# Experts' gate and up weights of a megabyte per transfer, their places released and awaited two pieces at a time

## The chip, the cores and the metric

One core of a Trainium2 chip runs the whole program in one launch. The metric is the device time of one execution in microseconds (us), the median over runs. The engines of the core are TensorE (PE; its weight loads are listed as PEld), VectorE (DVE), ScalarE (ACT), GpSimd (POOL) and SyncE (SP). Sixteen DMA engines move data between HBM and the core's SBUF; nearly all transfers of this kernel are issued by SP, in one queue.

## What is computed

The reference runs two blocks over 256 rows of width 1024, in float32. The first block has two layers, a retention mixer and a block attention mixer, each followed by a mixture of experts. The second has four layers (differential attention, HGRN2, chunked gating, differential attention), each with a cross attention and a dense SwiGLU. The change touches only the two mixtures of experts:

```python
def hier_moe(x, w_rg, b_rg, w_re, b_re, w_gate, w_up, w_down):
    ...                       # a router picks one of 4 groups and 2 of its 4 experts per row
    combine = (group_w[:, :, None] * within[:, None, :]).astype(x.dtype)
    y = jnp.zeros_like(t)
    for g in range(G):
        hg = jax.nn.silu(jnp.einsum('td,edf->tef', t, w_gate[g])) * jnp.einsum('td,edf->tef', t, w_up[g])
        y = y + jnp.einsum('tef,efd->td', hg * combine[:, g, :, None], w_down[g])
    return y.reshape(B, S, D)
```

Each layer has 16 experts with three matrices of 1024 by 512 numbers. All 16 experts' weights are read in each layer, 100.7 MB of float32, since some row may want any of them.

## The kernel before, in words

**Weights.** All "wide" weights come as blocks of 1024 by 512 numbers (2 MB). A block lies in HBM as four pieces (`WP = 4`), each 128 rows of 1024 numbers: 4 KB for each of the 128 partitions, 512 KB in all. In HBM the four pieces of a block stand one behind another, so that the same partition's rows of two neighbouring pieces are 512 KB apart. In SBUF a block fills 16 KB of each partition, piece behind piece. A "down" block is two such pieces (1 MB).

**Outside the experts** a block goes to `stage_w`, is split by ACT (`high_w`, line 748) and DVE (`low_w`, line 1179) and is then multiplied by PE (lines 2075 to 2077). SP issues a piece of the next block when the split has released the place (line 554).

**In a mixture of experts** the rows chosen by each expert are gathered, at most 64 for each (function `sparse`; another branch, `every`, takes over when an expert has more, and it does not run with these inputs). Experts go in 8 pairs, and the 512 hidden columns of an expert are done in two halves, so a layer has 16 steps, `v` = 0 to 15. A step needs, for both experts of the pair, the gate and up block of that half (`wide`, 4 MB together) and the down block (2 MB together). There are two sets of places: even steps use `proj` and `stage_w` (with `proj` and `stage_d` for down), odd steps `pair_w` and `pair_d`. PE does, in this order and in every step, `wide(v)` (line 2351; piece by piece, both experts side by side), inside it the transposes of the previous step's hidden values (line 2366) after the first piece, and in odd steps from 3 on a scatter (lines 2414 and 2415) before the third piece; then `down(v-1)` (line 2379). In early steps a gather (lines 2301 to 2310) and small products that weigh the slots (line 2326) follow.

**Order of the transfers.** SP works through one list written out by hand: in each layer `wide(v)` for v = 0 and 1 with their down blocks, then for v = 2 to 15 `wide(v)` and behind it, from v = 3 on, `down(v-1)`, then `down(15)`, then the first block of the stage that follows the experts, into `stage_w` (`load_wide` with `behind`). A transfer into a place waits until PE has used what lay there: `used_mw[i]` counts the pieces that PE has finished for expert `i`. For v = 0 and 1 the places belonged to the stage before, and the waits are on the splits (`split_lw`) or on PE (`used_w`). PE waits for a piece on `landed_mw[u][p]`, one semaphore for each piece number and each set, 16 for each expert's transfer. After the last step ACT and DVE split the first two pieces of the block that follows (lines 748 and 1179) before they keep the last pair's results (lines 878 and 1518), which PE then scatters (lines 2414, 2415) and DVE adds to `h` (line 1528).

`keep_clock` (line 2070) is a run of products whose result nobody reads.

Of the kernel before, what the change touches and what calls it, by code (L numbers as in the profile page):

```python
# [33 lines left out]
PIECE = 1024  # L34
WP = KC * WIDE // PIECE
# [23 lines left out]
PAIRS = ALL // 2  # L59
HALVES = MOE_UNITS // PAIRS // 2  # L60
# [213 lines left out]
def scatter_at(v):  # L274

    return (v - 3) // HALVES if v % HALVES and v >= 3 else None
# [38 lines left out]
def build(nc, dram, out):  # L315
    ctx = ExitStack()
    with ctx:
# [3 lines left out]
        def sem(name):  # L321
            return ctx.enter_context(nc.semaphore(name))
# [75 lines left out]
        def moe_wide(u, i):  # L398

            if u == 0:  # L400
                return stage_w[:, :] if i else proj[:, 0:WP * PIECE]
            return pair_w[i][:, :]
# [7 lines left out]
        def moe_x(r):  # L410
            return qk[:, 0:KC * S] if r % 2 == 0 else proj[:, X0:X0 + KC * S]
# [64 lines left out]
        split_hw, split_lw = sem("split_hw"), sem("split_lw")  # L476
        split_hd, split_ld = sem("split_hd"), sem("split_ld")
        used_w, used_d = sem("used_w"), sem("used_d")
# [38 lines left out]
        landed_mw = [[sem(f"landed_mw{u}{p}") for p in range(WP)] for u in range(HALVES)]  # L517
        landed_md = [[sem(f"landed_md{u}{p}") for p in range(DP)] for u in range(HALVES)]
        used_mw = [sem(f"used_mw{i}") for i in range(2)]
# [25 lines left out]
        def _(sp):  # L545
# [26 lines left out]
            def units_of(m, v):  # L572
                return [MOE_UNITS * m.moe + 2 * HALVES * (v // HALVES) + HALVES * i + v % HALVES for i in range(2)]

            def load_pair_wide(m, v, experts=range(2)):
                u, unit = v % HALVES, units_of(m, v)
                step, last = STEPS * m.moe + v, m.wide - 1
                for p in range(WP):
                    for i in experts:
                        if v >= HALVES:  # L580
                            sp.wait_ge(used_mw[i], WP * (step - HALVES) + p + 1)
                        elif u:
                            sp.wait_ge(used_w, WP * last + p + 1)
                        elif i:
                            sp.wait_ge(split_lw, WP * last + p + 1)
                        sp.dma_start(moe_wide(u, i)[:, p * PIECE:(p + 1) * PIECE],
                                     dram["wide"][m.wide + unit[i], p, :, :]).then_inc(landed_mw[u][p], 16)

            def load_pair_down(m, v, experts=range(2)):
                u, unit = v % HALVES, units_of(m, v)  # L590
# [11 lines left out]
            for s in PLAN:  # L602

                if s.kind == "residual" and moe_of(s) is not None:
                    m = PLAN[PLAN.index(s) + 3]
# [1460 lines left out]
        def _(pe):  # L2066
# [204 lines left out]
            def sparse(s):  # L2271
# [58 lines left out]
                def wide(v):  # L2330
                    q, u = v // HALVES, v % HALVES
                    e = q if q < 2 else q // 2 * 2 + 1
                    if v >= 2:
                        pe.wait_ge(way.gated, v - 1)
                    for p in range(WP):
                        if v == 0:
                            pe.wait_ge(way.first_kept, p + 1)
                        elif p == 0 and e:
                            pe.wait_ge(way.x_left, e)
                            pe.wait_ge(way.x_right, e)  # L2340
                        if v and p == 1:
                            turn_hidden(v - 1)
                        if p == 2 and scatter_at(v) is not None:
                            scatter(scatter_at(v), v)
                        pe.wait_ge(landed_mw[u][p], 32 * (PAIRS * s.moe + q + 1))
                        for k in range(KP):
                            c = KP * p + k
                            for i in range(2):
                                half = slice(i * SLOTS, (i + 1) * SLOTS)
                                x = c * S + q % 2 * P + i * SLOTS  # L2350
                                mm = pe.matmul(bank[4 + v % 2][half, :], moe_x(q // 2)[:, x:x + SLOTS],  # L2351
                                               moe_wide(u, i)[:, c * WIDE:(c + 1) * WIDE], start=c == 0, stop=c == KC - 1)
                                if k == KP - 1:
                                    mm.then_inc(used_mw[i], 1)
                        if v == 0 and p + 2 < WP:
                            gather_first(p + 2)

                def turn_hidden(v):
                    pe.wait_ge(way.gated, v + 1)
                    if v:  # L2360
                        pe.wait_ge(way.kept, v)
                    if v == 1:
                        pe.wait_ge(way.weights_kept, 1)
                    for c in range(DP):
                        o = GATED0 + FU + c * P
                        mm = pe.transpose(bank[6][:, c * P:(c + 1) * P], qk[:, o:o + P], ident[:, :])
                    mm.then_inc(way.turned, 1)
# [33 lines left out]
                def scatter(q, v):  # L2401
                    n = issued(gather_at, v)
                    pe.wait_ge(way.x_left, n)
                    pe.wait_ge(way.x_right, n)
                    pe.wait_ge(way.slots_kept, issued(turn_at, v))
                    if q:
                        pe.wait_ge(way.added, 4 * q)
                    for i, (t, half, b) in enumerate(scatter_order(q)):
                        if t == 0:
                            pe.wait_ge(way.z_low, 2 * q + half + 1)  # L2410
                        if i == 3 and q < PAIRS - 1:
                            pe.wait_ge(way.added, 4 * q + 1)
                        chosen = slots(q)[:, t * P:(t + 1) * P]
                        pe.matmul(b[:, :], chosen, z_high(half), start=True, stop=False)
                        pe.matmul(b[:, :], chosen, z_low(half), start=False, stop=True).then_inc(way.scattered, 1)
# [19 lines left out]
            def every(s):  # L2435
                way = ways[s.moe]
                steps = STEPS * s.moe

                def unit(q, u, i):
                    n = 2 * u + i  # L2440
                    for t in range(T):
                        x = slice(t * P, (t + 1) * P)
                        for p in range(WP):
                            pe.wait_ge(landed_mw[u][p], 32 * (q + (PAIRS * s.moe + 1)))
                            for k in range(KP):
                                c = KP * p + k
                                w = moe_wide(u, i)[:, c * WIDE:(c + 1) * WIDE]
                                pe.matmul(bank[4 + t][:, :], xhv[:, c, x].bitcast(F32), w, start=c == 0, stop=False)
                                mm = pe.matmul(bank[4 + t][:, :], xlv[:, c, x].bitcast(F32), w, start=False,
                                               stop=c == KC - 1)  # L2450
                            if t == T - 1:
                                mm.then_inc(used_mw[i], 1)
                    pe.wait_ge(way.gated, 2 * (2 * HALVES * q + (n + 1)))
                    for c in range(DP):
                        for t in range(T):
                            mm = pe.transpose(bank[6][:, c * S + t * P:c * S + (t + 1) * P],
                                              y[:, 512 + t * FU + c * P:512 + t * FU + (c + 1) * P], ident[:, :])
                    mm.then_inc(way.turned, 1)
                    pe.wait_ge(way.kept, 2 * HALVES * q + (n + 1))
                    for p in range(DP):  # L2460
                        pe.wait_ge(landed_md[u][p], 32 * (q + (PAIRS * s.moe + 1)))
                        for t in range(T):
                            for half in range(2):
                                mm = pe.matmul(bank[2 * t + half][:, :],
                                               qk[:, p * S + t * P:p * S + (t + 1) * P],
                                               moe_down(u, i)[:, p * PIECE + half * WIDE:][:, 0:WIDE],
                                               start=p == 0, stop=p == DP - 1)
                        mm.then_inc(used_md[i], 1)
                    pe.wait_ge(way.added, 4 * (2 * HALVES * q + (n + 1)))

                with pe.Fori(0, PAIRS) as q:
                    for u in range(HALVES):
                        for i in range(2):
                            unit(q, u, i)
# [466 lines left out]
```

## Time and profile before

| | us |
|---|---|
| median of 3 runs | 2607.13 (2606.32 to 2611.19) |
| the profiled execution, its own time | 2608.18 |
| its span, first to last instruction | 2606.4 |
| PE busy in the span | 2511.2 (96%) |
| weight loads of PE | 1862.3 (71%) |
| DVE busy | 1314.2 (50%) |
| ACT busy | 1072.6 (41%) |
| DMA queue of SP, share of the 16 engines | 56.5% |

The profile is of one execution. The first mixture of experts lies at about 241 to 481 us of the span, the second at about 622 to 860 us. The table is an average over stages with different limits. A DMA engine that works without a gap reads as a share of about 1.03 in this profile.

### The profile page before, as it was taken

To read this page: it belongs to the slowest core of one execution; us is meant where nothing else is said; L and a number is where in the kernel's file an instruction comes from. 1 tells how busy PE (TensorE), PEld (TensorE's weight loads), DVE (VectorE), ACT (ScalarE), POOL (GpSimd) and SP (SyncE) were. 2 spreads that over 40 slices of the span, in tenths; PEclk is the share of its full clock that TensorE was granted. 3 is DMA by queue.
4 is the path that set the end of the run, shared out by engine and by line. 5 is a ranking of instruction groups with operands and counts; after the bars stand their busy time and mean duration, and the time that the engine had idled before them with its cause. 6 is when DMAs were issued, how large, how long until landed. Compare 5 with 4: busy or idle time off the path is not lost.

```text
span 2606.4 us, 32925 instructions
## 1 busy us (share of the span) xinstructions
PE 2511.2 (96%) x11944; PEld 1862.3 (71%) x11944; DVE 1314.2 (50%) x1945; ACT 1072.6 (41%) x1640; POOL 55.0 (2%) x87
## 2 busy tenths in 40 slices
PE   8999998899998899999999999999999999999998
PEld 6876433586442578878888887888788888788887
DVE  5654111563121566555547756555656555665554
ACT  4453111352111454454455445444444444544443
POOL 0000000000000000000000000000000000000000
PEclk9999999999999999999999999999999999999999
DMA  7548999638999534365543255554545554343653
GB/s 237 192 142 331 377 409 409 237 130 339 382 409 409 188 130 164 125 209 186 189 152 115 65 177 170 186 188 175 169 162 177 186 193 154 130 155 117 229 184 106
DMA packets 149983, 546.14 MB, mean 210 GB/s; under 512 B 17047, under 2 KB 17248, under 8 KB 149736
## 3 DMA queue, kind: packets, MB, share of 16 engines
q1 hardware_dynamic: 144664, 526.04, 56.5%
q0 software_dynamic: 4912, 17.43, 2.2%
q8 instruction: 79, 1.29, 0.2%
q10 hardware_dynamic: 288, 1.05, 0.1%
q14 instruction: 40, 0.33, 0.0%
HBM read 543.39 MB, written 2.63 MB: 209 GB/s over the span
## 4 chain that ended last, share of the span: by engine, by line
PE 81%; DVE 7%; DMA 5%; ACT 3%; issue 3%; POOL 1%; SPq 0%; ACTq 0%; DVEq 0%; POOLq 0%
PE bank L2075 20%; PE bank L2077 19%; PE bank L2076 19%; PE bank L2351 7%; PE bank L2379 3%; DMA stage_w<-in_wide 2%; PE bank L2154 2%; DVE low_w L1179 2%; DMA pair_w<-in_wide 1%; DMA pair_d<-in_down 1%; PE bank L2753 1%; PE bank L2670 1%; ACT tmp L997 1%; PE bank L2640 1%; DVE y L1233 1%
## 5 line engine op out<-in xcount | busy, mean ns | idle before, releaser
L2075 PE MATMUL bank<-high_w,xh 128*128 128x512 f32 x2112 | 842.4, 399 | 23.9 <-DVE xl L1194 9.6
L1179 DVE TENSOR_TENSOR low_w<-stage_w,high_w 128x1024 fp32r<-128x1024 f32 x528 | 641.2, 1223 | 399.4 <-ACT high_w L748 374.1
L2077 PE MATMUL bank<-high_w,xl 128*128 128x512 f32 x2112 | 825.6, 391 | 0.0
L2076 PE MATMUL bank<-low_w,xh 128*128 128x512 f32 x2112 | 824.8, 391 | 0.0
L748 ACT ACTIVATE high_w<-stage_w 128x1024 fp32r<-128x1024 f32 x528 | 555.2, 1059 | 215.6 <-PE bank L2077 184.2
L2075 PEld LDWEIGHTS bank<-high_w,xh 128*128 128x128 f32 x2112 | 397.9, 188 | 118.9 <-issue 21.3
L2077 PEld LDWEIGHTS bank<-high_w,xl 128*128 128x128 f32 x2112 | 397.8, 188 | 84.9
L2076 PEld LDWEIGHTS bank<-low_w,xh 128*128 128x128 f32 x2112 | 398.5, 189 | 77.9
L1537 DVE TENSOR_TENSOR qk<-qk,bank 128x256 f32<-128x256 f32 x32 | 13.5, 421 | 225.9 <-ACT qk L886 225.9
L2075 PE MATMUL bank<-high_d,hidden_h 128*128 128x512 f32 x320 | 124.9, 390 | 0.0
L2077 PE MATMUL bank<-high_d,hidden_l 128*128 128x512 f32 x320 | 124.6, 389 | 0.0
L2076 PE MATMUL bank<-low_d,hidden_h 128*128 128x512 f32 x320 | 124.5, 389 | 0.0
L1616 DVE TENSOR_TENSOR hidden_l<-bank,hidden_h 128x512 fp32r<-128x512 f32 x40 | 27.7, 692 | 191.0 <-ACT hidden_h L953 191.0
L953 ACT ACTIVATE hidden_h<-bank 128x512 fp32r<-128x512 f32 x40 | 23.9, 598 | 216.3 <-PE bank L2496 216.3
L1187 DVE TENSOR_TENSOR low_d<-stage_d,high_d 128x1024 fp32r<-128x1024 f32 x88 | 104.2, 1222 | 15.7 <-ACT high_d L757 15.7
L886 ACT ACTIVATE qk<-bank 128x256 f32<-128x256 f32 x32 | 12.3, 383 | 190.5 <-PE bank L2351 190.5
L757 ACT ACTIVATE high_d<-stage_d 128x1024 fp32r<-128x1024 f32 x88 | 88.5, 1052 | 5.1 <-PE bank L2077 5.1
L763 ACT ACTIVATE xh<-bank 128x512 fp32r<-128x512 f32 x88 | 47.3, 593 | 102.1 <-PE bank L2154 102.1
L656 POOL TENSOR_TENSOR stat<-stat,minus_half 128x1 f32<-128x1 f32 (+3 forms) x49 | 34.9, 712 | 2504.4 <-DVE stat L1215 1971.4
L1194 DVE TENSOR_TENSOR xl<-bank,xh 128x512 fp32r<-128x512 f32 x88 | 56.3, 683 | 55.0 <-ACT xh L763 55.0
L780 ACT ACTIVATE y<-h 128x1024 f32<-128x1024 f32 x37 | 39.2, 1059 | 104.4 <-DVE stat L1174 75.2
L788 ACT ACTIVATE proj<-bank 128x512 f32 (+1 forms) x50 | 29.9, 598 | 118.9 <-PE bank L2077 118.7
(315 smaller groups left out, 2794.8 us busy)
## 6 DMA issues: line engine op xcount, KB each, us to landing
stage_w<-in_wide SPq DMA_DIRECT2D x592, 512.0 KB, 4.4
pair_w<-in_wide SPq DMA_DIRECT2D x128, 512.0 KB, 13.5
stage_d<-in_down SPq DMA_DIRECT2D x120, 512.0 KB, 4.4
proj<-in_wide SPq DMA_DIRECT2D x64, 512.0 KB, 13.0
pair_d<-in_down SPq DMA_DIRECT2D x64, 512.0 KB, 14.6
proj<-in_down SPq DMA_DIRECT2D x32, 512.0 KB, 14.3
gain<-in_gains POOLq DMA_DIRECT2D x19, 512.0 KB, 4.9
skew<-bias_dram POOLq DMA_DIRECT2D x1, 1536.0 KB, 16.6
```

The source lines that it names most:

```text
L748: act.activation(high_w[:, w], stage_w[:, w], ACT.Copy).then_inc(split_hw, 1)
L757: act.activation(high_d[:, w], stage_d[:, w], ACT.Copy).then_inc(split_hd, 1)
L763: act.activation(part(xhv, b, chunk), part_bank(b), ACT.Copy).then_inc(kept_h, 1)
L1179: vec.tensor_tensor(low_w[:, w], stage_w[:, w], high_w[:, w].bitcast(F32), ALU.subtract)\
L1187: vec.tensor_tensor(low_d[:, w], stage_d[:, w], high_d[:, w].bitcast(F32), ALU.subtract)\
L1194: vec.tensor_tensor(part(xlv, b, chunk), part_bank(b), part(xhv, b, chunk).bitcast(F32), ALU.subtract).then_inc(kept_l, 1)
L2075: pe.matmul(o, hi, wh, start=start, stop=False)
L2076: pe.matmul(o, hi, wl, start=False, stop=False)
L2077: return pe.matmul(o, lo, wh, start=False, stop=stop)
L2154: mm = pe.transpose(bank[2 * t + i][:, k * P:(k + 1) * P], rows[:, t, (4 * i + k) * P:(4 * i + k + 1) * P], ident[:, :])
L2351: mm = pe.matmul(bank[4 + v % 2][half, :], moe_x(q // 2)[:, x:x + SLOTS], moe_wide(u, i)[:, c * WIDE:(c + 1) * WIDE], start=c == 0, stop=c ...
L2379: mm = pe.matmul(bank[side][half, :], qk[:, HIDDEN0 + p * P:][:, half], moe_down(u, i)[:, p * PIECE + side * WIDE:][:, 0:WIDE], start=u == ...
```

## The change

The two pieces p and p+1 of an expert's gate and up block become one transfer of 1 MB, with p = 0 and 2. It waits for the release of both pieces, and counts on the semaphore of the first of them. PE waits on that semaphore for both pieces. Down blocks and all other weights keep their transfers of 512 KB.

```diff
             def load_pair_wide(m, v, experts=range(2)):
                 u, unit = v % HALVES, units_of(m, v)
                 step, last = STEPS * m.moe + v, m.wide - 1
-                for p in range(WP):
+                for p in range(0, WP, 2):
                     for i in experts:
                         if v >= HALVES:
-                            sp.wait_ge(used_mw[i], WP * (step - HALVES) + p + 1)
+                            sp.wait_ge(used_mw[i], WP * (step - HALVES) + p + 2)
                         elif u:
-                            sp.wait_ge(used_w, WP * last + p + 1)
+                            sp.wait_ge(used_w, WP * last + p + 2)
                         elif i:
-                            sp.wait_ge(split_lw, WP * last + p + 1)
-                        sp.dma_start(moe_wide(u, i)[:, p * PIECE:(p + 1) * PIECE],
-                                     dram["wide"][m.wide + unit[i], p, :, :]).then_inc(landed_mw[u][p], 16)
+                            sp.wait_ge(split_lw, WP * last + p + 2)
+                        sp.dma_start(moe_wide(u, i)[:, p * PIECE:(p + 2) * PIECE].rearrange("p (a n) -> p a n", a=2),
+                                     dram["wide"][m.wide + unit[i], p:p + 2, :, :].rearrange("a p n -> p a n"))\
+                            .then_inc(landed_mw[u][p], 16)
...
-                        pe.wait_ge(landed_mw[u][p], 32 * (PAIRS * s.moe + q + 1))
+                        pe.wait_ge(landed_mw[u][p - p % 2], 32 * (PAIRS * s.moe + q + 1))
...
-                            pe.wait_ge(landed_mw[u][p], 32 * (q + (PAIRS * s.moe + 1)))
+                            pe.wait_ge(landed_mw[u][p - p % 2], 32 * (q + (PAIRS * s.moe + 1)))
```

The second of the two PE waits is in the branch `every`.

## Rows read from the trace of the kernel before

**Rows 1.** The page, GB/s moved in 40 equal slices of the span (65.2 us each).
```profile
GB/s 237 192 142 331 377 409 409 237 130 339 382 409 409 188 130 164 125 209 186 189 152 115 65 177 170 186 188 175 169 162 177 186 193 154 130 155 117 229 184 106
```

**Rows 2.** Chain that ended last, 403 to 520 us: start us, us, what.
```profile
410.28 16.26 DMA pair_w<-in_wide
...
458.75 15.22 DMA stage_w<-in_wide
...
474.04 1.07 ACT high_w L748
...
478.51 0.47 PE bank L2414
```

**Rows 3.** The same chain, 787 to 900 us, the second mixture of experts.
```profile
837.38 15.25 DMA stage_w<-in_wide
```

**Rows 4.** Windows: stretch, length, PE, PEld, DVE, ACT, POOL busy, clock, DMA share, GB/s.
```profile
276.00:280.00 4.00, 4.00 (x16) 1.22 (x16) 0.52 (x1) 0.77 (x2) 0.00 (x0) 0.79 0.13 29
280.00:288.00 8.00, 8.00 (x39) 2.60 (x36) 0.42 (x1) 0.38 (x1) 0.00 (x0) 1.00 0.99 362
288.00:294.00 6.00, 6.00 (x36) 3.16 (x36) 2.00 (x3) 2.52 (x5) 0.00 (x0) 1.00 1.03 420
...
296.00:470.00 174.00, 165.90 (x761) 60.99 (x761) 32.69 (x56) 21.23 (x48) 0.00 (x0) 1.00 1.03 409
676.00:850.00 174.00, 166.40 (x764) 60.90 (x760) 31.85 (x55) 21.59 (x48) 0.00 (x0) 1.00 1.03 409
...
656.00:658.00 2.00, 2.00 (x9) 0.43 (x6) 0.00 (x0) 0.05 (x1) 0.00 (x0) 0.87 0.01 2
```

**Rows 5.** Timeline of SP's queue, 244 to 345 us: start, us, line, what, count.
```profile
278.84 0.33 SPq L586 DMA_DIRECT2D proj<-in_wide  x1
...
281.07 0.33 SPq L586 DMA_DIRECT2D proj<-in_wide  x1
...
286.22 2.52 SPq L598 DMA_DIRECT2D pair_d<-in_down  x4
292.12 8.79 SPq L586 DMA_DIRECT2D pair_w<-in_wide  x8
...
318.55 8.79 SPq L586 DMA_DIRECT2D pair_w<-in_wide  x8
```

**Rows 6.** Timeline of SP's queue in the second mixture of experts.
```profile
657.99 0.33 SPq L586 DMA_DIRECT2D proj<-in_wide  x1
...
660.22 0.33 SPq L586 DMA_DIRECT2D proj<-in_wide  x1
```

**Rows 7.** Timeline of SP's queue, 400 to 495 us.
```profile
425.64 1.08 SPq L586 DMA_DIRECT2D proj<-in_wide  x1
```

**Rows 8.** Timeline of PE, 454 to 476 us, idle before and its releaser in brackets.
```profile
454.91 1.94 PE L2351 MATMUL bank<-pair_w,proj 128*64 128x512 f32 x8 [0.35 <-DMA pair_w<-in_wide]
...
461.42 3.65 PE L2351 MATMUL bank<-pair_w,proj 128*64 128x512 f32 x16
...
472.74 2.79 PE L2393 MATMUL bank<-pair_d,qk 128*64 128x512 f32 x12 [0.94 <-DMA pair_d<-in_down]
```

**Rows 9.** Timeline of ACT, 464 to 492 us.
```profile
475.32 1.06 ACT L748 ACTIVATE high_w<-stage_w 128x1024 fp32r<-128x1024 f32 x1 [0.22 <-DMA stage_w<-in_wide]
476.28 1.25 ACT L878 ACTIVATE xl<-bank,tmp 128x512 fp32r<-128x512 f32 x2
```

**Rows 10.** The page's DMA issues: out<-in, queue, count, size, median us to landing.
```profile
pair_w<-in_wide SPq DMA_DIRECT2D x128, 512.0 KB, 13.5
...
tmp<-in_mem POOLq DMA_DIRECT2D x1, 1024.0 KB, 8.2
```

**Rows 11.** Windows (columns as Rows 4) while the transfer of `in_mem` is under way.
```profile
870.00:872.00 2.00, 2.00 (x6) 0.81 (x5) 1.35 (x2) 0.00 (x0) 0.29 (x1) 1.00 1.00 406
```

**Rows 12.** Windows (columns as Rows 4) around pauses of PE.
```profile
480.00:485.00 5.00, 2.24 (x7) 1.02 (x6) 4.18 (x8) 2.19 (x4) 0.56 (x1) 1.00 0.34 111
...
618.00:620.00 2.00, 1.05 (x7) 0.95 (x7) 1.63 (x9) 1.17 (x2) 0.00 (x0) 0.75 0.74 297
```

## The prediction

> **What bounds the kernel now.** I read the page first. PE is busy for 96% of the span, and everywhere outside the experts the transfers are far from full. The slices of GB/s show the exception: in each mixture of experts two slices in a row read 409 and the slices around them 331 to 382 [rows 1]. So I went to windows over those two stretches. For 174 us in each of them the DMA engines work at a share of 1.03, which in this profile is no gap at all, and move 409 GB/s [rows 4]. PE is busy for 166 of the 174 us there, so the two are close, and the next question is which of them ends last. The chain of waits answers it. From 410 us on it runs through transfers of 15 to 16 us each (that is the time from issue to landing, spent mostly in the queue), and it leaves the experts through the first piece of `stage_w` that follows: issued at 458.75, landed at 474.0, split by ACT, and only then the last scatter at 478.51 [rows 2]. The second mixture ends in the same way, with 15.25 us for that transfer [rows 3].
>
> The balance explains it. A step needs 12 transfers of 524,288 bytes, 6.29 MB, which at 409 GB/s is 15.4 us. PE's own step is shorter: SP's issues for `pair_w`, released by PE's first piece, come at 292.12 and 318.55, two steps apart, so 13.2 us a step [rows 5]. PE starts with a lead of places already filled, eats it up at 2.2 us a step, and from 410 us on waits for landings. The end of the stage is then the time when the queue last began to work, plus the bytes behind that time at 409 GB/s. That beginning can be seen: from 276 to 280 us the engines are nearly idle (share 0.13), because both sets of places are full and PE is still in step 2's first piece. At 278.84 PE has finished that piece and SP issues the first transfer for step 4 [rows 4, 5]. Behind it stand 12 pairs of wide blocks of 4 MiB, 13 down pairs of 2 MiB and half a MiB for `stage_w`, 74.5 MiB, at 2.56 us each 191 us. Data starts near 280 and the landing is at 474.0, 194 us later, so the queue has indeed not run dry again. In the second mixture the engines stand at share 0.01 in 656 to 658 us and the same issue comes at 657.99 [rows 4, 6].
>
> **The change, part by part.**
>
> *Release by two pieces.* The transfer for step 4 now waits until PE has finished the second piece of step 2. The time of that release is in the trace, since SP issues the second piece there: 281.07 instead of 278.84, 2.23 us later [rows 5]. It is what PE needs for the transposes and one more piece. In the second mixture it is 660.22 instead of 657.99, again 2.23 us [rows 6]. The engines are idle in just this time, so it is paid in full. Does the queue run dry again later? The new order puts 4 MiB of step 4 in from about 282.0, done at 292.3, then down(3), issued from 286.22, done at 297.4. The next release, step 5 at the second piece of step 3, comes at about 292.12 + 2.23 = 294.35 [rows 5]. That leaves 3.0 us of work in the queue, and since PE then releases places in 13.2 us for which the queue needs 15.4, the margin only grows. Earlier releases (steps 0 to 3) come later by up to 3 us too, but these transfers end before the idle stretch at 276 us, and PE needs step 3 only at 290, so I cost them at nothing; their cover is that idle stretch of 3.5 us. In the full phase the places are not what SP waits for: an issue takes 1.08 us there against 0.33 with a short queue [rows 5, 7], so SP is held back by the queue and the coarser release is free. Cost: 2.23 us in each mixture, 4.46 us in all.
>
> *Arrival by two pieces.* PE now needs both experts' first 1 MiB, so its first piece starts one MiB later than before, 2.56 us. While PE has a lead this costs nothing. At the end it matters. In step 15 the first piece starts at 454.91 on its landing and the last two pieces end at about 465.1 [rows 8]. With the first start near 457.4 they end near 467.5, down(14) near 471.4, and after transposes and one idle product the last down products start at about 472.6 instead of waiting until 472.74 for half of them [rows 8]. Their first half, which ACT's L878 waits for, is then finished at about 474.5 instead of 473.7. But L878 starts at 476.28, behind the split of the second `stage_w` piece, which starts at 475.32 on its landing [rows 9]. So 1.8 us remain, and I cost this part at zero. If that cover were gone it would cost at most the 0.8 us.
>
> *Fewer and larger transfers.* Eight of a step's 12 transfers become 4. No row shows a 1 MiB transfer of SP's queue, so the rate is bounded from both sides. Above: 420 GB/s in 288 to 294 us, with pieces of the old size, right behind a stretch of 362 in 280 to 288 [rows 4]; it looks like engines that had fallen behind and catch up, so it is an end and not a value. Below: 362, the poorest stretch with work queued. I take the 409 that both mixtures hold for 174 us with 512 KB [rows 4], since an engine that shows no gap has no fixed cost left to save. The start could also move: the first 8 us at 362 instead of 409 lose 0.9 us, and a fuller queue may avoid that; on the other side a transfer of twice the rows may take longer to start, by at most the 0.9 us that pass from issue to data. That is 1.3 to 3.1 us a mixture around 2.23.
>
> The Trainium skill, "DMA: Bandwidth & Descriptors", section "Measured (HBM→SBUF, 128 partitions, SWDGE, issued from GpSimd)", says to batch transfers to at least 1 MiB. By its fit of about 2.0 us plus the bytes at 436 GB/s a lone transfer of 512 KB would reach 163 GB/s and one of 1 MiB 238. By that rule the change would be a gain; the trace's 409 GB/s with 512 KB shows that the fixed part is hidden as long as several are queued.
>
> The same page, in section "iDMA fabric — 4 AXI ports for 8 engines, asymmetric across TPBs", gives 408.7 GB/s for a stream of 1 MiB transfers with 4 KB rows from SP, which would leave the sum as it is; no run here shows it yet.
>
> *Instructions.* SP has fewer issues and waits, PE the same number of waits, every second of them already satisfied. Nothing here is on the path.
>
> **Sum.** 2608.18 (the profiled execution) + 4.46 = 2612.6. That execution lies 1.05 us above the median of the runs, 2607.13, so the forecast for the median is 2607.13 + 4.46 = 2611.6, slower by 0.17%. What a measurement of this kernel can tell from no change is about 0.2%, or 5.2 us.
>
> **Rivals.**
>
> *A: the larger transfers raise the rate (faster).* If the full phase ran at 420 instead of 409, a step would take 15.0 us instead of 15.4, over some 12 steps 4.8 us less in each mixture. Against 2.23 more, the balance is -2.6 us a mixture, 2602 us. It decides from about 414 GB/s on, where the rate pays the late start. For it: the row at 420. Against it: no gap in the engines at 409, and the number of 4 KB rows stays. 12%.
>
> *B: the late start is not paid (no change).* The end is bound by the queue, but the poor first 8 us and a rate of a few GB/s more could give back the 2.23 us, or the idle stretch is a little shorter than it looks. 2607 to 2608. Also here the case that something between DMA and the last scatter has slack that the chain doesn't show. Against it: ACT begins the split within 0.1 us of the landing [rows 2]. 14%.
>
> *C: the source pattern costs rate (slower).* A partition's two rows now come from places 512 KB apart, in turn. For it nothing in the trace. Against it: the one transfer of the kernel with just this pattern, `in_mem` on POOL's queue, 1 MiB [rows 10], runs in a window at 406 GB/s with share 1.00 [rows 11]. If it cost 3% on the two thirds of the bytes, it would be 0.3 us a step, 3.7 us a mixture, so 2619. 6%. The Trainium skill, "DMA: Bandwidth & Descriptors", section "Latency and other measured facts", has a rule that speaks against the change here, on copies whose row pitch is a large power of two; at 512 KB it gives 207 GB/s against 214 in full, the 3% from which it would come out like C.
>
> *D: PE's clock falls (slower).* PE's pauses in the waiting phase get longer, up to some 3 us at the start of a step instead of several of about 0.7. A pause of 2.8 us within 480 to 485 us left the granted clock at 1.00, but in 618 to 620 us, with PE busy for 1.05 of 2 us, it fell to 0.75 in the window, on the way to the lower of its two levels, 1.2 GHz [rows 12]. If that comes in the last step of a mixture, where PE has some 2 us of slack, PE loses about half of 7 us, so 1.5 us each after the slack, up to 2615 with the late start. It decides only in the last 15 us of a mixture; earlier the 2.2 us of slack in each step take it up. 10%.
>
> **How the numbers follow.** Forecast 58% (own range 2609.5 to 2613.5), A 12%, B 14%, C 6%, D 10%. Within the forecast the bound of 2612.3 cuts off the upper third. Faster by over 0.2%: most of A, 10%. Slower: a third of the forecast (19%), C, most of D, 34% in all. Same: the rest, 56%. The range holds the forecast, B, D and the milder half of A and leaves out the far ends of A and C: 2602 to 2618.
>
> **What would show it.** Right: in the profile after, SP's first 1 MiB issue into `proj` for step 4 lies at about 281.1 and 662.4 (the second with the first mixture's delay), the window 276 to 282 us is emptier, the full phase reads 409 GB/s, PE waits about one step earlier than 410 us, and the first `stage_w` piece behind the experts lands near 476.2. Wrong: a rate away from 409 in the full phase, a second idle stretch near 297 us (the margin of 3.0 us misjudged), a start of L878 that follows the last down products and not the split, or a lower clock between 440 and 476 us.

## The result

| | us, median | runs | ratio to the kernel before, 95% interval |
|---|---|---|---|
| before | 2608.94 | 20 | |
| changed kernel | 2614.05 | 20 | 1.0020 (1.0014 to 1.0027) |
| changed kernel, measured again later | 2615.52 | 11 | 1.0021 (1.0012 to 1.0030) |

The change makes the kernel slower by 0.2%, 5.1 us between the medians and 3.7 to 7.0 us by the interval. The forecast was 4.5 us slower.

The page of the changed kernel has the same two full slices (409) in each mixture of experts as before, and no more than before in the two slices ahead of them: 319 and 367 where it was 331 and 377, and in the second mixture 302 and 381 where it was 339 and 382 [rows 1]. The second line is of its DMA issues, the gate and up blocks of `pair_w`, now half as many of 1 MB, with 15.5 us from issue to landing.
```profile
GB/s 235 193 141 319 367 409 409 244 142 302 381 409 409 222 130 146 131 208 193 193 138 128 66 169 169 186 184 185 162 161 178 193 192 154 129 153 117 231 186 104
...
pair_w<-in_wide SPq DMA_DIRECT2D x64, 1024.0 KB, 15.5
```

The place to look is SP's queue at the start of a mixture. To compare two executions a common mark is needed, since they have drifted apart by some us before the experts begin. The mark is the moment at which PE has used step 0's first piece. In the trace before, SP issues a transfer for step 2 there, and the one for the second piece 2.96 us later:
```profile
245.58 0.33 SPq L586 DMA_DIRECT2D proj<-in_wide  x1
...
248.54 0.33 SPq L586 DMA_DIRECT2D proj<-in_wide  x1
```
In the trace after, the same timeline (start, us, line, what) has its first release only behind the second piece, 250.46, so the mark is 250.46 - 2.96 = 247.50. PE's own timeline agrees: the products that follow the first piece of step 0 begin 0.09 us before the mark in both kernels, at 245.49 before and 247.41 after. So this execution is 1.9 us later than the one before at the mark. That isn't the change: in the second profile of the same kernel the mark is at 245.06, 0.5 us earlier than before. In the next fence the second row is the release for step 4. The last row, in a fence of its own, is the release for step 4 in the second mixture.
```profile
250.46 0.38 SPq L586 DMA_DIRECT2D proj<-in_wide  x1
...
282.98 0.38 SPq L586 DMA_DIRECT2D proj<-in_wide  x1
```
```profile
665.09 0.38 SPq L586 DMA_DIRECT2D proj<-in_wide  x1
```
From the mark to step 4's release it was 278.84 - 245.58 = 33.26 us before [rows 5] and is 282.98 - 247.50 = 35.48 us now: 2.22 us later, where 2.23 was forecast. Windows of the changed kernel (columns as in rows 4) show that the DMA engines move nothing in that time, and that behind it the full phase has its old rate in both mixtures:
```profile
280.00:282.00 2.00, 2.00 (x12) 0.61 (x10) 0.00 (x0) 0.38 (x1) 0.00 (x0) 1.00 0.00 0
282.00:288.00 6.00, 6.00 (x32) 2.00 (x30) 0.42 (x1) 0.38 (x1) 0.00 (x0) 1.00 0.62 229
...
296.00:470.00 174.00, 163.98 (x748) 61.77 (x748) 33.26 (x56) 20.82 (x46) 0.00 (x0) 0.98 1.03 409
...
664.00:666.00 2.00, 2.00 (x12) 0.71 (x10) 0.00 (x0) 0.00 (x0) 0.00 (x0) 1.00 0.00 0
676.00:850.00 174.00, 162.56 (x742) 60.85 (x740) 31.42 (x54) 21.20 (x47) 0.00 (x0) 0.98 1.03 409
```
The chain of waits leaves the first mixture as before, through the first `stage_w` piece and ACT's split of it, now at 477.42:
```profile
462.14 15.21 DMA stage_w<-in_wide
477.42 1.06 ACT high_w L749
```
From step 4's release to this split it is 194.4 us, and it was 195.2 before; in the second mixture 194.6 (to 859.70) and 194.7. So the end of a mixture follows the release of step 4 at a fixed distance. From the mark to the split each mixture has grown by 1.5 us (first: 228.5 to 229.9) and 2.1 us (second: 228.0 to 230.1).

The single profiled execution does not show this as a plain 3.6 us. At the split of the second mixture it is 7.0 us late: 1.9 of it from before the first mark, 1.5 and 2.1 in the mixtures, 1.5 between them. The last lies at PE's clock at 488 us, where `keep_clock`'s eight products take 1.7 us longer than in the kernel before (first fence after, second before):
```profile
486.53 5.40 PE L2071 MATMUL bank<-ident 128*128 128x512 f32 x8 [2.54 <-issue]
```
```profile
483.33 3.70 PE L2070 MATMUL bank<-ident 128*128 128x512 f32 x8 [2.76 <-issue]
```
The rest of the program then ran 3.3 us shorter than before. In the second profile of the same kernel it ran 1.5 us longer. These are differences of single executions, and they are the reason why what follows rests on distances inside a mixture and on the ratios.

**The arrival by two, at the end of a mixture.** PE's timeline in the first mixture: step 15 begins on its landing after a pause of 2.36 us, and the last down products run without waiting for a landing. ACT's timeline: its L879 still comes directly behind the split of the second piece.
```profile
460.88 1.94 PE L2352 MATMUL bank<-pair_w,proj 128*64 128x512 f32 x8 [2.36 <-DMA pair_w<-in_wide]
...
475.41 3.65 PE L2394 MATMUL bank<-pair_d,qk 128*64 128x512 f32 x16
```
```profile
478.71 1.06 ACT L749 ACTIVATE high_w<-stage_w 128x1024 fp32r<-128x1024 f32 x1 [0.23 <-DMA stage_w<-in_wide]
479.68 1.25 ACT L879 ACTIVATE xl<-bank,tmp 128x512 fp32r<-128x512 f32 x2
```
In the second mixture the pause is 2.87 us and the clock falls behind it: the eight products take 3.27 us instead of 1.94, the windows read 0.62 and 0.53, and at the end ACT waits 0.18 us for PE's last down products instead of going on directly.
```profile
843.15 3.27 PE L2352 MATMUL bank<-pair_w,proj 128*64 128x512 f32 x8 [2.87 <-DMA pair_w<-in_wide]
```
```profile
842.00:844.00 2.00, 0.85 (x2) 0.32 (x4) 0.27 (x1) 0.00 (x0) 0.00 (x0) 0.62 1.03 410
844.00:846.00 2.00, 2.00 (x8) 0.53 (x4) 0.00 (x0) 0.00 (x0) 0.00 (x0) 0.53 1.02 406
```
```profile
862.80 0.69 ACT L879 ACTIVATE xl<-bank,tmp 128x512 fp32r<-128x512 f32 x1 [0.18 <-PE bank L2394]
```
In the second profile of the changed kernel this wait is 0.44 us, also in the second mixture:
```profile
859.96 0.69 ACT L879 ACTIVATE xl<-bank,tmp 128x512 fp32r<-128x512 f32 x1 [0.44 <-PE bank L2394]
```
That is rival D, at the place that it named, at a price of 0.2 to 0.4 us.

The clock falls in the first mixture too, where the transfers hide it. Behind a pause of 1.98 us at the start of step 14 two windows read 0.63 and 0.52, with the DMA engines at their full share:
```profile
445.52 0.61 PE L2352 MATMUL bank<-proj 128*64 128x512 f32 x1 [1.98 <-DMA stage_w<-in_wide]
```
```profile
446.00:448.00 2.00, 2.00 (x8) 0.33 (x4) 0.00 (x0) 0.00 (x0) 0.00 (x0) 0.63 1.03 410
448.00:450.00 2.00, 2.00 (x8) 0.82 (x8) 0.00 (x0) 0.38 (x1) 0.00 (x0) 0.52 1.04 410
```
There are four such falls in this execution, from about 416, 446, 812 and 843 us, and they are why both full windows read 0.98 where the kernel before reads 1.00 [rows 4]. Only the last one reaches ACT.

### The profile page after: what moved, and what is told of

Read it like the earlier page. It is cut to its first block, busy times and chain, and to the rows that moved or that the text cites. A ratio compares the mean times of both kernels' runs of the same rounds, so it can differ in the third digit from the quotient of the medians.

```text
span 2610.1 us, 32797 instructions
## 1 busy us (share of the span) xinstructions
PE 2511.3 (96%) x11944; PEld 1863.7 (71%) x11944; DVE 1314.3 (50%) x1945; ACT 1072.4 (41%) x1640; POOL 55.0 (2%) x87
## 4 chain that ended last, share of the span: by engine, by line
PE 80%; DVE 7%; DMA 7%; ACT 3%; issue 3%; SPq 1%; POOL 0%; ACTq 0%; DVEq 0%; POOLq 0%
PE bank L2076 20%; PE bank L2078 19%; PE bank L2077 19%; PE bank L2352 7%; DMA stage_w<-in_wide 4%; PE bank L2380 2%; DMA pair_w<-in_wide 2%; PE bank L2155 2%; DVE low_w L1180 2%; PE bank L2754 1%; PE bank L2671 1%; PE bank L2641 1%; ACT tmp L998 1%; DVE y L1234 1%; PE bank L2071 1%
## 6 DMA issues: line engine op xcount, KB each, us to landing
pair_w<-in_wide SPq DMA_DIRECT2D x64, 1024.0 KB, 15.5
```

## The experiments

Theory L: a mixture ends when the DMA engines last ran dry, plus the bytes behind that point at 409 GB/s; the release by two moves that point. Its rivals are the arrival in lumps and PE's clock (P), the large transfers themselves (R, S), and PE's own work as the bound (Q). Each ratio is against the kernel before, run beside it, with 6 to 12 executions of each variant and 20 of the changed kernel.

| kernel | release of step 4, first and second mixture | release to split | ratio (95%) |
|---|---|---|---|
| before | 278.84, 657.99 | 195.2, 194.7 | |
| changed | 282.98, 665.09 | 194.4, 194.6 | 1.0020 (1.0014 to 1.0027) |
| release by two only | 281.89, 663.84 | 194.3, 195.4 | 1.0022 (1.0013 to 1.0031) |
| release by four only | 284.28, 672.77 | 195.4, 195.8 | 1.0049 (1.0033 to 1.0064) |
| arrival by two only | 277.76, 659.57 | 194.3, 194.6 | 0.9997 (0.9988 to 1.0007) |
| 1 MB from step 6 | 278.74, 660.19 | 194.8, 194.7 | 1.0007 (0.9997 to 1.0018) |

The releases are on each execution's own clock; the third column is the distance from there to ACT's split of the block behind the experts. In six kernels and twelve mixtures it stays within 194.3 to 195.8 us. These are single executions, so a difference of 1 us in it can't be put down to an edit.

**1. Only the release by two**

```diff
-sp.wait_ge(used_mw[i], WP * (step - HALVES) + p + 1)
+sp.wait_ge(used_mw[i], WP * (step - HALVES) + p - p % 2 + 2)
```
(and the same for `used_w` and `split_lw`; transfers and PE's waits as before)

> Only the release by two pieces: transfers stay at 512 KB and PE still waits piece by piece. Theory L (late start: the last idle stretch of the DMA engines ends when step 4's first transfer is released, and that comes 2.23 us later in each mixture): slower by 4.5 us against the kernel before (ratio 1.0017), with the release in the first mixture one piece later and the window behind it empty for 2 us more. Theory P (arrival in lumps lengthens PE's pauses, its clock falls, and that is what costs): no change, 0 us, and no fall of the clock in the waiting phase.

Measured 2615.38 us, ratio 1.0022, 5.7 us by the ratio (3.4 to 8.1). The whole loss is there without any large transfer. Its mark is 246.40 and step 4's release (SP's timeline, then the split in ACT's) is 35.49 us behind it, as in the changed kernel. PE's clock does not fall in the full phase of either mixture (1.00 in both windows). From the mark to the split the mixtures grow by 1.3 and 2.9 us:
```profile
281.89 0.33 SPq L586 DMA_DIRECT2D proj<-in_wide  x1
```
```profile
476.19 1.06 ACT L748 ACTIVATE high_w<-stage_w 128x1024 fp32r<-128x1024 f32 x1 [3.69 <-DMA stage_w<-in_wide]
```

**2. Only the arrival by two**

```diff
-pe.wait_ge(landed_mw[u][p], 32 * (PAIRS * s.moe + q + 1))
+if p % 2 == 0:
+    pe.wait_ge(landed_mw[u][p], 32 * (PAIRS * s.moe + q + 1))
+    pe.wait_ge(landed_mw[u][p + 1], 32 * (PAIRS * s.moe + q + 1))
```

> Only the arrival by two pieces: transfers of 512 KB, released piece by piece, but PE starts a pair of pieces only when both have landed. Theory L: no change (0 us, at most 0.8 us a mixture), because the last down products have 1.8 us of slack before ACT needs them. Theory P: slower by 2 to 5 us, with pauses of PE of 2 to 3 us in the waiting phase and a lower granted clock there.

Measured 2608.92 us, ratio 0.9997 (3.1 us faster to 1.8 slower): no change, as L says. PE pauses for 2.75 us at the start of step 15 (its timeline), and ACT's split stands 194.3 us behind the release:
```profile
455.54 1.94 PE L2353 MATMUL bank<-pair_w,proj 128*64 128x512 f32 x8 [2.75 <-DMA pair_w<-in_wide]
```
```profile
277.76 0.33 SPq L586 DMA_DIRECT2D proj<-in_wide  x1
```
```profile
472.09 1.06 ACT L748 ACTIVATE high_w<-stage_w 128x1024 fp32r<-128x1024 f32 x1 [2.39 <-DMA stage_w<-in_wide]
```
P's pauses came and its price did not. The expected fall of the clock did not come in this execution either: eight products after 2.75 us of pause took 1.94 us, the normal time. In other executions it probably did: the mean granted clock over the 12 executions is 0.9906, against 0.9926 for the kernel before beside it, and the time is the same all the same.

This trace also shows how far single executions differ. The first mixture's release stands 31.64 us behind the mark (246.12) here, 1.6 us less than before, though the edit doesn't touch it: the clock read 0.97 in the window 276 to 278 us, where the kernel before had 0.59.

**3. Large transfers from step 6 on**

```diff
+FROM = 6
...
-for p in range(WP):
+pieces = 2 if v >= FROM else 1
+for p in range(0, WP, pieces):
...
-    sp.wait_ge(used_mw[i], WP * (step - HALVES) + p + 1)
+    sp.wait_ge(used_mw[i], WP * (step - HALVES) + p + pieces)
```
(with the transfer of one or two pieces to match, and PE's wait on the first of two from step 6 on)

> Transfers of 1 MB only from step 6 on; steps 0 to 5 keep 512 KB and the release piece by piece, so the queue starts as early as before and is never dry after that. It has the large transfers and the arrival in lumps without the late start. Theory L: no change (within 1 us). Theory P: slower by 2 to 5 us. Theory R (the large transfers change the rate of the full phase): the window from 296 to 470 us reads other than 409 GB/s; 1% of it would be 1.7 us a mixture.

Measured 2610.05 us, ratio 1.0007 with an interval that holds 1. The full phase has the old rate, so R falls (windows). PE's clock did fall here in step 15, after a pause of 2.87 us, with eight products in 2.58 us (PE's timeline):
```profile
296.00:470.00 174.00, 164.68 (x752) 61.10 (x752) 32.60 (x56) 21.21 (x47) 0.00 (x0) 0.98 1.03 409
```
```profile
456.66 2.58 PE L2361 MATMUL bank<-pair_w,proj 128*64 128x512 f32 x8 [2.87 <-DMA pair_w<-in_wide]
```
The same transfers without the late start cost 1.8 us by the point estimate, a third of what the change costs; the interval goes from 0.8 us faster to 4.7 slower, so the times alone don't show that they cost nothing. The trace has no growth: from the marks (247.11 and 626.92) to the splits it is 226.4 and 228.0 us, where the kernel before had 228.5 and 228.0. That the large transfers aren't what costs rests on this and on experiment 1, where the whole loss came without them.

**4. The dose raised: release by four**

```diff
-sp.wait_ge(used_mw[i], WP * (step - HALVES) + p + 1)
+sp.wait_ge(used_mw[i], WP * (step - HALVES) + WP)
```

> The dose doubled and more: transfers of 512 KB, but from step 2 on a place of the gate and up weights is released only when PE has used all four pieces. In the trace before, the fourth piece of step 2 is done at about 284.5 us and the first at 278.84, so theory L expects 5.7 us in each mixture, 11.3 us in all (ratio 1.0043). Theory P: no change.

Measured 2622.81 us, ratio 1.0049, 12.8 us by the ratio (8.6 to 16.7), where 11.3 were expected. Counted from the end of step 0, which SP's issue for the fourth piece shows in both traces (253.21 before, 254.62 here), the two mixtures grow by 4.2 and 6.7 us. The split follows the later release again:
```profile
284.28 0.33 SPq L586 DMA_DIRECT2D proj<-in_wide  x1
```
```profile
479.65 1.06 ACT L748 ACTIVATE high_w<-stage_w 128x1024 fp32r<-128x1024 f32 x1 [3.70 <-DMA stage_w<-in_wide]
```

**5 to 7. The dry stretch filled from the other side.** If L holds, the kernel gains when PE reaches step 2 sooner. What the gathers of steps 1 and 2 deliver is first needed in step 4:

```diff
-    return {0: 1, 1: 2, 2: 3, 4: 4, 6: 5, 8: 6, 10: 7}.get(v)
+    return {0: 1, 2: 2, 3: 3, 4: 4, 6: 5, 8: 6, 10: 7}.get(v)
...
-                    if issued(scatter_at, v):
-                        pe.wait_ge(way.added, 4 * issued(scatter_at, v))
+                    if issued(scatter_at, v + 1):
+                        pe.wait_ge(way.added, 4 * issued(scatter_at, v + 1))
```
(the second edit, in `gather`, lets the gather of step 3 wait for the scatter ahead of it)

> The kernel before, with the gathers of step 1 and step 2 moved to steps 2 and 3 (the same work, later), so that PE reaches step 2 about 3.4 us earlier and releases step 4's places before or just as the queue runs dry at 276 us. Theory L: the idle stretch of about 3.5 us shrinks to under 1 us and the end of each mixture comes about 3 us earlier, so faster by 5 to 7 us, about 2602. Rival Q (the end is bound by PE's own work in each mixture, the start only shifts it): no change, since PE does the same work.

Measured 2606.84 us, ratio 0.9986 (0.9973 to 0.9998); repeated later beside other kernels, it read 2603.66 us and 0.9983:

> The kernel before with two gathers moved, once more, beside the two others: faster than before by 3 to 4 us as in its first comparison, and slower than the kernel with three gathers moved by 2 us or more.

So 3.6 and 4.4 us faster by the ratios, less than the 5 to 7 expected the first time; the upper end of both intervals, 7.0 and 7.6, reaches into it, and by the trace the two mixtures are 4.0 and 2.6 us shorter. Its mark is 247.01 and the release (SP's timeline) 29.69 us behind it instead of 33.26; the dry stretch is nearly gone (window), and the split (ACT's) is 224.4 us behind the mark instead of 228.5:
```profile
276.70 0.33 SPq L586 DMA_DIRECT2D proj<-in_wide  x1
```
```profile
276.00:278.00 2.00, 2.00 (x8) 0.63 (x8) 0.00 (x0) 0.38 (x1) 0.00 (x0) 0.77 0.93 344
```
```profile
471.44 1.06 ACT L748 ACTIVATE high_w<-stage_w 128x1024 fp32r<-128x1024 f32 x1 [3.69 <-DMA stage_w<-in_wide]
```
In the second mixture the same distance is 225.4 us against 228.0. Q falls: PE's work is the same and the end came earlier.

The changed kernel with the same edit, and the changed kernel once more beside it:

> The changed kernel with the same two gathers moved. Its first release for step 4 then comes about 3.4 us earlier too, at about 277.6 us, while its queue runs dry at about 277.3. Theory L: the coarse release is paid only as far as the queue is dry, so this kernel lies 1 to 3 us above the one with only the gathers moved, in both mixtures together, instead of the 4.5 us between before and after; about 2604. Rival S (a price of the large transfers that has nothing to do with the idle stretch): the full 4.5 us remain between the two.

> The changed kernel again, beside the two others on the same chip: slower than before by about 5 us, as in its first comparison (ratio 1.002), and above the kernel with the gathers moved by the sum of both effects.

Measured 2610.20 us (ratio 1.0000, 0.9991 to 1.0009) and 2615.52 us. The gathers moved give the changed kernel 5.3 us and the kernel before 3.1 (medians of executions side by side). Between the two with moved gathers there remain 3.4 us, more than the 1 to 3 expected and less than the 5.5 between the two without. The release came where it was expected: at 282.35, 32.1 us behind the mark (29.1 behind the second piece's, and 2.96), which on the clock of the kernel before is 277.7. The queue was empty by then for about 1 us (window), against at most 0.3 us in the kernel before with the gathers moved. From the mark to the split this kernel takes 226.6 and 227.2 us, the other 224.4 and 225.4, and 225.5 and 225.7 when repeated. L's 1 to 3 us and the 4.5 us of rival S, a price of the large transfers of their own, are too close for this pair:
```profile
282.35 0.38 SPq L586 DMA_DIRECT2D proj<-in_wide  x1
```
```profile
282.00:284.00 2.00, 2.00 (x12) 0.70 (x10) 0.00 (x0) 0.00 (x0) 0.00 (x0) 1.00 0.56 184
```

**8 and 9. Also the first gather one step later**

```diff
-    return {0: 1, 1: 2, 2: 3, 4: 4, 6: 5, 8: 6, 10: 7}.get(v)
+    return {1: 1, 2: 2, 3: 3, 4: 4, 6: 5, 8: 6, 10: 7}.get(v)
```
(the wait in `gather` as in 5, and in step 1 the gather ahead of the products that weigh the slots, on PE and DVE)

> The kernel before, with the gathers of steps 0, 1 and 2 each moved one step later (and in step 1 ahead of the products that weigh the slots). PE then begins step 1 about 3.8 us earlier than in the kernel before, and the first release for step 3 comes at about 255 us instead of 258.85, before the queue runs dry at 258.3. Theory L (a mixture ends when the engines last ran dry, plus the bytes behind): the dry stretch at 258 to 260 us goes too, the queue is deeper at 276 us, and each mixture ends 1 to 3 us earlier than with only two gathers moved; faster than before by 6 to 12 us, about 2600. Rival Q (PE's own work bounds a mixture): same as the kernel before.

> The changed kernel (1 MB transfers, release and arrival by two) with the same moves. Theory L: where the queue no longer runs dry before step 4, the coarse release costs little; 0 to 3 us above the kernel that has only the moves, against the 5 us between before and after. Rival S (a price of the large transfers of their own): 4 to 5 us above it.

Measured 2607.75 us (0.9987, 0.9976 to 0.9997), and 2611.82 us (1.0008, 0.9996 to 1.0020) for the changed kernel. The 6 to 12 us were a misreading of my own theory. The dry stretch before step 3 did go, but only the last one counts: step 3's bytes came earlier, the queue ran dry earlier, and step 4's release stood where it stood with two gathers moved, since PE has the same work before it. SP's timeline and the window:
```profile
277.67 0.33 SPq L586 DMA_DIRECT2D proj<-in_wide  x1
```
```profile
276.00:278.00 2.00, 2.00 (x10) 0.35 (x6) 0.00 (x0) 0.00 (x0) 0.00 (x0) 0.65 0.09 37
```
The release is 30.1 us behind its mark of 247.54, against 29.7 and 30.9 in the two runs with two gathers moved. The kernel with two gathers moved, beside it, was expected to be slower by 2 us or more and was 4.1 us faster (2603.66), so the third move gained nothing.

The changed kernel lies 4.1 us above its partner, where L had 0 to 3 and rival S 4 to 5. By the number S did better. But L's condition wasn't met: the release of step 4 is 34.0 us behind the mark in this kernel, 3 to 4 us later than in its partner, and the split stands 194.4 us behind it in both mixtures, as everywhere. So the expectation had the dry stretch wrong again, and the pair doesn't speak for S.

**10 and 11. The weighing products behind the first piece of step 2**, with the two gathers as in 5:

```diff
+                        if v == 2 and p == 1:
+                            weigh_slots()
                         if v and p == 1:
                             turn_hidden(v - 1)
...
-                    if v == 1:
-                        weigh_slots()
```

> The kernel before, with two gathers moved as before (steps 1 and 2 to 2 and 3) and the products that weigh the slots (4.2 us of PE) moved behind the first piece of step 2. Step 4's release then comes some 7 us earlier than in the kernel before, at about 272 us on its clock, before the queue runs dry at 276. Theory L: the last dry stretch is then the one before step 3's release at 258.85, with 80.5 MiB behind it, 207 us with the start; each mixture ends about 6 us earlier than in the kernel before and 3 us earlier than with only the gathers moved. Faster by 8 to 14 us, about 2597. Rival Q (PE's work bounds a mixture once the queue is full): no better than the 3 to 7 us of the kernel with the gathers moved.

> The changed kernel with the same moves. Theory L: the coarse release is now paid at step 3's first release, one piece later, 2 us in each mixture; 3 to 5 us above the kernel with the moves and 512 KB transfers. Were the queue never dry after step 2's release, the two would be equal.

Measured 2602.25 us (0.9979, 0.9966 to 0.9992), and 2609.57 us (0.9999, 0.9989 to 1.0009) for the changed kernel. The first is the fastest median of the study, 7.2 us under the kernel before, though short of the 8 to 14 expected. SP's timeline shows why: step 4's first release did come at 268.92, but the second, behind the moved products, at 276.96, and one MiB did not last so long (window). From that second release, with 1 MiB less behind it, the split is 193.2 us away:
```profile
268.92 0.33 SPq L586 DMA_DIRECT2D proj<-in_wide  x1
...
276.96 0.33 SPq L586 DMA_DIRECT2D proj<-in_wide  x1
```
```profile
276.00:278.00 2.00, 2.00 (x10) 0.61 (x8) 0.00 (x0) 0.00 (x0) 0.00 (x0) 0.91 0.80 289
```
From the mark to the split it is 225.8 and 225.3 us in the two mixtures, no better than with the gathers alone (225.5 and 225.7 in the repeated run); the ratios 0.9979 and 0.9983 don't tell the two apart. By the time alone that is what rival Q expected here as well; against Q stands run 5, and for L the dry window above. Its mean granted clock was higher too, 0.9940 against 0.9922 for the kernel before beside it, so part of its lead may be clock. The changed kernel with this edit can't use the first piece alone, so its release stays behind both and behind the products; 7.3 us lie between the two medians, more than the 3 to 5 expected. By the traces it is 1.2 and 2.0 us in the two mixtures; the rest I can't place.

## Why the prediction was right

**The bound.** It held: the end of each mixture follows step 4's release at 194.3 to 195.8 us in the changed kernel and in all four that isolate or enlarge a part of it. The arithmetic of 74.5 MiB at 409 GB/s had given 191, without the time from the issue to the first data.

**The late start.** 2.23 us forecast, 2.22 us read in the changed kernel. Alone it gives the whole loss (1.0022), and raised to four pieces it gives 1.0049. The next release, that of step 5, was forecast at 294.35 and came at 296.27, which less the 1.9 us is the same place, and the feared second dry stretch near 297 us isn't there (share 1.03 from 294 to 300). What reaches the end of a mixture is 1.5 and 2.1 us. The first mixture has 0.8 us less from release to split than before. The working had allowed 0.9 us for a fuller queue, but the same 194.3 stands in the run with only the arrival by two, whose queue is as before, so this can be the spread of single executions.

**The arrival.** Costed at nothing, measured at nothing (0.9997). Its cover, ACT's split, was still there in the first mixture and used up, with 0.2 to 0.4 us over, in the second, where the clock had fallen. PE's waits for landings begin earlier by two steps and not by one: its first is at 416.34 in the kernel before and at 389.16 in the changed one. (The 410 of the prediction is the issue of a transfer that PE later waits for [rows 2], and no wait of PE.) It cost nothing, since these steps have slack.

**The transfers' size.** The rate stayed at 409 GB/s in both mixtures, so rivals A and C are out. Two rows 512 KB apart in turn cost nothing that shows. B is out as the whole answer; its part about the start of the queue is not shown.

**Rival D** happened, and cost little. Two of the signs that the prediction called wrong did come: a lower clock between 440 and 476 us (0.63 and 0.52 at 446 to 450), and, in the second mixture, L879 behind the last down products. The prediction held because of the price and not because the clock stood. It had put 10% on D and the price at 1.5 us a mixture, from 7 us at the lower clock with 2 us of slack. The fall in the last step is over within two windows of 2 us, half of that time, so the loss is some 1.7 us (estimate, from clocks of 0.62 and 0.53 in two windows of 2 us), and all but 0.2 to 0.4 us of it went into slack.

**The number.** 2611.6 against 2614.05. Of the 2.4 us between them 1.8 are the kernel before, whose median over 20 runs is 2608.94 and not 2607.13. So 2614.05 lies 0.5 us above the forecast's own range (2609.5 to 2613.5), and it is the starting point that does it. The loss itself is 5.1 and 5.5 us in two comparisons, the forecast 4.5, the distances in the traces 3.6 and 3.5. Each interval is 3 to 5 us wide, so that the number comes within 1 us is in part luck.

Most of the scatter goes with PE's clock. Over the 108 executions of the kernel before in the four groups of experiments, time and mean granted clock go together (correlation -0.86), 2.4 us longer for each 0.001 less. With this slope, an estimate, the two kernels that change only the release can be brought to the clock of the kernel beside them: the mean of release by two is 6.4 us above it at a clock lower by 0.0010, which leaves 4.0, and that of release by four 13.9 at 0.0011, which leaves 11.3; expected were 4.5 and 11.3. For the changed kernel this doesn't work, because its four falls are in phases where the transfers set the time. By the windows around them, again an estimate, they make up 0.0026 of the 0.0029 by which its mean clock is lower than that of the kernel before (0.9891 and 0.9920 in the second comparison).

## What to carry to other kernels

Where a queue of transfers is the bound, look for the last moment at which it was empty; what released the first transfer behind it sets the end of the stage, however long the stage is. A coarser release showed no cost while the queue was deep (from step 6 on), and was paid in full there. So keep the small pieces for the first transfers behind the dry point, or move other work of the releasing engine behind the release: that gave 3.4 to 5.5 us here by the ratios, on the kernel with the small transfers.

## What was not expected

SP's time for an issue grows with the size of the transfer when the queue is full, so nothing is gained there. In the waiting phase of the changed kernel (SP's timeline) an issue of 1 MB mostly takes 2.2 to 2.4 us, and one of 512 KB took 1.08 [rows 7]; with a short queue the issues into `proj` take 0.38 and 0.33.
```profile
430.08 2.36 SPq L586 DMA_DIRECT2D proj<-in_wide  x1
```
PE's clock reacts to a pause at one time and not at another. A pause of 2.87 us was followed by 3.27 us for eight products in the changed kernel and by 2.58 us with large transfers from step 6 on; in that same execution another pause of 2.87 us, at 807.61, was followed by the normal 1.94 us, as was one of 2.75 us with the arrival by two alone:
```profile
807.61 1.94 PE L2361 MATMUL bank<-pair_w,proj 128*64 128x512 f32 x8 [2.87 <-DMA pair_w<-in_wide]
```
